# A two-layer decoder on one core: output projections, norms, the second attention's entry and the place of the weight splits

## What is computed

```python
def rms_norm(x):
    y = x * lax.rsqrt(jnp.mean(x * x, axis=-1, keepdims=True) + NORM_EPS)

for i in range(DEPTH):                                   # 2
    shift, scale, gate = silu(c) @ ada_w[i, 0] + ada_b[i, 0]   # three parts of 1024
    h = rms_norm(x) * (1.0 + scale) + shift
    y = forgetting_attention(h, ...) if i == 0 else latent_attention(h, ...)
    x = x + gate * y
    shift, scale, gate = silu(c) @ ada_w[i, 1] + ada_b[i, 1]
    h = rms_norm(x) * (1.0 + scale) + shift
    x = x + gate * conv_gated_mlp(h, ...)                # 1024 -> 2 x 2816 -> 1024
return rms_norm(x) * final_g

def latent_attention(h, w_a, g_q, g_kv, w_uq, w_ukv, w_o):
    c_q, c_kv, k_rope = jnp.split(h @ w_a, [384, 384 + 256], axis=-1)
    c_q, c_kv = rms_norm(c_q) * g_q, rms_norm(c_kv) * g_kv
    q = c_q @ w_uq       # 16 heads of 64 + 32 (rotated)
    kv = c_kv @ w_ukv    # 16 heads of 64 keys + 64 values; k_rope, rotated, is shared by all heads
    ...                  # causal softmax by blocks of 128 queries
    return o @ w_o
```

## Time and profile before

| | us |
|---|---|
| median of 3 runs (1350.25 to 1352.49) | 1351.91 |
| profiled execution | 1351.14 |
| its span | 1349.3 |

### The profile page before, as it was taken

One profiled execution on the slowest core, in us unless ns is written; L12 is line 12 of the kernel. 1 busy time (PEld: TensorE's weight loads), 2 busy tenths in 40 slices (PEclk: granted clock), 3 DMA queues, 4 the chain that ended last, 5 costly groups with the idle time before them and its releaser, 6 DMA issues.

```text
span 1349.3 us, 17962 instructions
## 1 busy us (share of the span) xinstructions
PE 1281.7 (95%) x6209; PEld 999.3 (74%) x6209; DVE 832.1 (62%) x1262; ACT 543.2 (40%) x970; POOL 9.6 (1%) x23
## 2 busy tenths in 40 slices
PE   6999999988999999999989899989899999999997
PEld 3677777666888888888867566657678888888886
DVE  3656656666888878755355666664666666663332
ACT  5544444424333333322233566553444344432222
POOL 2000000000000000000000000000000000000000
PEclk7999999997999999999979899989899999999998
DMA  9523333352556656556322111122233333333332
GB/s 307 174 63 102 118 94 94 97 185 70 182 191 195 196 176 199 161 179 193 118 76 47 34 30 35 33 72 63 63 94 93 96 102 97 93 89 102 99 90 72
DMA packets 230600, 154.29 MB, mean 114 GB/s; under 512 B 27773, under 2 KB 221778, under 8 KB 227474
## 3 DMA queue, kind: packets, MB, share of 16 engines
q1 hardware_dynamic: 230546, 153.55, 37.9%
HBM read 151.43 MB, written 2.10 MB: 114 GB/s over the span
## 4 chain that ended last, share of the span: by engine, by line
PE 86%; DVE 5%; ACT 3%; issue 2%; DMA 2%; SPq 2%; ACTq 0%; DVEq 0%
PE pj L1415 74%; PE ov L1687 3%; PE tr L1659 2%; PE sc L1643 2%; PE sc L1631 1%; DMA ada_w_sb<-in_ada_w_dram 1%; SPq L459 1%; DVE wl L966 1%; ACT wh L606 1%; DVE nmax L1120 1%; DMA first_ada<-in_ada_w_dram 1%; PE ov L1481 1%; DVE ada_w_sb L1013 1%; PE sc L1649 0%; PE ov L1573 0%
## 5 line engine op out<-in xcount | busy, mean ns | idle before, releaser
L966 DVE TENSOR_TENSOR wl<-raw,wh 128x1024 fp32r<-128x1024 f32 (+2 forms) x214 | 234.4, 1095 | 311.4 <-ACT wh L606 310.4
L1415 PE MATMUL pj<-hh,wh 128*128 128x512 f32 x992 | 402.1, 405 | 21.7 <-issue 7.0
L606 ACT ACTIVATE wh<-raw 128x1024 fp32r<-128x1024 f32 (+2 forms) x214 | 204.4, 955 | 473.2 <-PE pj L1415 473.2
L1415 PE MATMUL pj<-hh,wl 128*128 128x512 f32 x992 | 391.1, 394 | 0.0
L1415 PE MATMUL pj<-hl,wh 128*128 128x512 f32 x992 | 390.8, 394 | 0.0
L1415 PEld LDWEIGHTS pj<-hh,wh 128*128 128x128 f32 x992 | 188.6, 190 | 71.0 <-issue 16.3
L1415 PEld LDWEIGHTS pj<-hh,wl 128*128 128x128 f32 x992 | 188.8, 190 | 40.5
L1415 PEld LDWEIGHTS pj<-hl,wh 128*128 128x128 f32 x992 | 189.3, 191 | 35.8 <-DVE hl L1044 0.5
L1415 PE MATMUL pj<-gh,wh 128*128 128x512 f32 x512 | 204.3, 399 | 9.4 <-ACT tmp L797 7.2
L1415 PE MATMUL pj<-gh,wl 128*128 128x512 f32 x512 | 200.5, 392 | 0.0
L1415 PE MATMUL pj<-gl,wh 128*128 128x512 f32 x512 | 200.5, 392 | 0.0
(11 more groups left out here) (173 smaller groups left out, 1033.1 us busy)
## 6 DMA issues: line engine op xcount, KB each, us to landing
raw<-in_ffn_w_in_dram SPq DMA_DIRECT2D x88, 512.0 KB, 3.8
ada_w_sb<-in_ada_w_dram SPq DMA_DIRECT2D x40, 1024.0 KB, 5.1
raw<-in_ffn_w_out_dram SPq DMA_DIRECT2D x32, 448.0 KB, 3.6
raw<-in_fox_w_in_dram SPq DMA_DIRECT2D x24, 512.0 KB, 3.8
first_ada<-in_ada_w_dram SPq DMA_DIRECT2D x16, 512.0 KB, 8.9
raw<-in_ffn_w_out_dram SPq DMA_DIRECT2D x16, 512.0 KB, 3.9
raw<-in_fox_w_o_dram SPq DMA_DIRECT2D x8, 512.0 KB, 4.1
raw<-in_mla_w_o_dram SPq DMA_DIRECT2D x8, 512.0 KB, 3.8
```

The source lines that it names most:

```text
L606: act.activation(wh[:, n0 % 2, 0:kt, :], raw[:, n0 % 2, 0:kt, :], ACT.Copy).then_inc(w_hi, 1)
L966: dve.tensor_tensor(wl[:, n0 % 2, 0:kt, :], raw[:, n0 % 2, 0:kt, :], f32(wh[:, n0 % 2, 0:kt, :]), ALU.subtract).then_inc(w_lo, 1)
L1415: ins = pe.matmul(bank_[:, :], (wl if term == 2 else wh)[:, s, kt, :], (rl if term == 1 else rh)(kt), start=start and j == 0, stop=stop an ...
```

## The change

Seven edits.
1. Two more slices of w_ada (ten instead of eight) are done in the first attention, at other steps, and their DMAs move with them; PE's sum of the first group moves to an earlier step. In the first projection two are left, at tiles 0 and 3.
2. In both projections the first tile's residual comes ahead of the low part on DVE (`ahead`), and PE waits only for the residual, not for ACT's square.
3. `norm_over` gets ten products of constants (2, 3 and 5) into a bank that nothing reads.
4. Entry: query latents ahead of the rotated key on DVE; the spread in the middle of chunk C_KR; PE's first chunk follows the low parts tile by tile; the wait for POOL's copies moves to the second head.
5. MLA loop: the splits move from the end of b = 2 and b = 3 to their beginning, on ACT and DVE.
6. In the last pair of heads, the split of b = 3 moves to step 8.
7. `MLA_FILL` shifts one product each in two steps.

```diff
-ADA_OUT = ADA_END[1] - DT // 2
+ADA_OUT = {0: ADA_END[1] - 2, 3: ADA_END[1] - 1}
...
-MLA_FILL = (0, 3, 7, 11, 15, 19, 22, 33, 33)
+MLA_FILL = (0, 3, 7, 11, 15, 18, 21, 33, 33)
...
-FOX_ADA = {(i, 4 * j + 3): 2 * i + j for i in range(PAIRS // 2) for j in range(2)}
-FOX_ADA_LOAD = {(0, 5): 2, (1, 2): 3, (1, 5): 4, (2, 2): 5, (2, 5): 6}
-FOXO_ADA_LOAD = {2: 7, 3: 8, 4: 9, 5: 10, 6: 11}
+FOX_ADA = {(n // 8, n % 8): p for p, n in enumerate((3, 7, 10, 12, 15, 19, 22, 24, 27, 31))}
+FOX_ADA_LOAD = {(0, 5): 2, (1, 2): 3, (1, 3): 4, (1, 5): 5, (2, 2): 6, (2, 5): 7}
+FOXO_ADA_LOAD = {0: 8, 2: 9, 3: 10, 4: 11}
...
             act.activation(early[:, 7:8], eps[:, 0:1], ACT.Exp)
-            act.wait_ge(mm, C_KR + 1)
             latents_hi(QRT, KVRT)
+            split(C_KR + 2)
             act.wait_ge(kr, 2)
             act.activation(k32(0)[MQ:P, :], k32(0)[HD:MQ, :], ACT.Copy).then_inc(ev_a, 1)
-            split(C_KR + 2)
...
                 v = turned_unit(t, s)
+                if fill and b == 2:
+                    split_after(n0, t, 4, nxt)
+                if fill and b == 3 and nxt is None:
+                    split_after(n0 + 1, t, 4, nxt)
...
-                if fill and b == 2:
-                    split_after(n0, t, 4, nxt)
                 if fill and b == 3:
                     act.wait_ge(tr_r, R + (MLA_TR * j + 2))
                     mla_take_v(t * 4 + (n0 + 1))
-                    split_after(n0 + 1, t, 4, nxt)
+                if nxt is not None and s == 8:
+                    split(C_MLAO + 1)
...
-                def step(i, j, nxt):
-                    if nxt is None or j == 0:
+                def step(i, j, nxt, ahead=False):
+                    late = ahead or (nxt is not None and j == 1)
+                    if not late:
                         split_after(C + j, i, 2, nxt)
                     dve.wait_ge(mm, i * 2 + (C + j + 1))
-                    residual(i * 2 + j, j, i * 2 + (T + j), (T + j) % 2, k, norm_n)
-                    if nxt is not None and j == 1:
+                    add(i * 2 + j, (T + j) % 2, k)
+                    if late:
                         split_after(C + j, i, 2, nxt)
+                    square_add(i * 2 + j, j, i * 2 + (T + j), norm_n)
...
+            dve.wait_ge(ev_d, T_KR)
+            latents_pre(QRT, N_CQ, V_GQ)
+            latents_lo(QRT, KVRT)
+
             kt = tmp[:, 5, :]
...
+            split(C_KR + 2)
+            dve.wait_ge(kr, 1)
             dve.wait_ge(ev_d, T_KR + 1)
-            latents_pre(QRT, N_CQ, V_GQ)
-            dve.wait_ge(kr, 1)
             dve.tensor_tensor(k32(0)[HD:MQ, :], kt[0:ROPE, :], rope_sb[0:ROPE, :], ALU.add).then_inc(kr, 1)
-            latents_lo(QRT, KVRT)
-            split(C_KR + 2)
...
                 n0 = C_MLA + 2 * (j + 1)
+                if fill and b == 2:
+                    split_after(n0, t, 4, nxt)
+                if fill and b == 3 and nxt is None:
+                    split_after(n0 + 1, t, 4, nxt)
                 if s < 8:
                     maximum(s, t * 8 + (U_MLA + s), b)
...
                 mean_most(n)
+                idle_products(2)
                 mean_last(n, tile_n)
+                idle_products(3)
                 spread(n)
+                idle_products(5)
+
+            def idle_products(count):
+
+                for _ in range(count):
+                    pe.matmul(SC[0][:, :], sel[:, 0, :], sel[:, 0:QB, :], start=True, stop=True)
...
-                if (i, w) == (2, 1):
+                if (i, w) == (1, 6):
                     ada_sum(0)
...
                 def step(i, j):
-                    bank_free(i * 2 + (T + j))
+                    pe.wait_ge(ev_d, i * 2 + (T + j - 1))
                     product(C + j, i, 2, 0, 3 * DT, g_h, g_l, PJ[(T + j) % 2])
...
-            product(C_KR, 0, 0, 12, 3 * DT, h_h, h_l, PJ[T_KR % 2])
+            product(C_KR, 0, 0, 12, 15, h_h, h_l, PJ[T_KR % 2])
             spread(N_CQ)
+            product(C_KR, 0, 0, 15, 3 * DT, h_h, h_l, PJ[T_KR % 2])
...
-            pe.wait_ge(cn_lo, QRT + KVRT)
             bank_free(T_MLA)
-            product(C_MLA, 0, 0, 0, 3 * QRT, uq_h, uq_l, PJ[T_MLA % 2])
-            bank_free(T_MLA + 1)
+            for kt in range(QRT):
+                pe.wait_ge(cn_lo, KVRT + kt + 1)
+                product(C_MLA, 0, 0, 3 * kt, 3 * kt + 3, uq_h, uq_l, PJ[T_MLA % 2])
+            pe.wait_ge(ev_d, T_KR + 1)
             product(C_MLA + 1, 0, 0, 0, 3 * KVRT, ukv_h, ukv_l, PJ[(T_MLA + 1) % 2])
-            pe.wait_ge(kr_twin, 2)
...
+                    if first(t) and s == QB:
+                        pe.wait_ge(kr_twin, 2)
```

More of the change, by code:

```diff
@@ L1176, in residual, with add @@
             def residual(m, j, tile_n, bk, k, norm_n):
+                add(m, bk, k)
+                square_add(m, j, tile_n, norm_n)
+            def add(m, bk, k):
                 g = mod[:, k, 2 * DT + m:2 * DT + m + 1] if isinstance(m, int) else \
@@ L1181, in residual, with square_add @@
                                          op0=ALU.mult, op1=ALU.add).then_inc(ev_d, 1)
+            def square_add(m, j, tile_n, norm_n):
                 if isinstance(m, int) and m == DT - 1:
@@ L1198, in dense @@
                     for n in range(DT - 2):
-                        step(n // 2, n % 2, None)
-                        if ADA_OUT + n < ADA_END[1]:
-                            ada_step(ADA_OUT + n)
-                else:
-                    with dve.Fori(0, DT // 2 - 1) as i:
+                        step(n // 2, n % 2, None, n == 0)
+                        if n in ADA_OUT:
+                            ada_step(ADA_OUT[n])
+                else:
+                    for j in range(2):
+                        step(0, j, None, j == 0)
+                    with dve.Fori(1, DT // 2 - 1) as i:
                         for j in range(2):
@@ L1374, in mla_step @@
                     mla_take_k(t * 4 + (n0 + 1), 1 - j)
-                    split_after(n0, t, 4, nxt)
-                if fill and b == 3:
-                    split_after(n0 + 1, t, 4, nxt)
+                if nxt is not None and s == 8:
+                    split(C_MLAO + 1)
             for s in range(8):
```

## The result

| | before | after |
|---|---|---|
| median of 4 runs, us | 1351.35 (1350.25 to 1352.49) | 1329.86 (1328.97 to 1331.30) |
| profiled execution, its span | 1351.14, 1349.3 | 1328.97, 1327.2 |

The changed kernel takes 0.9842 of the time before (95% interval 0.9825 to 0.9859), 21.5 us less; a second series, beside other runs of the kernel before, gave 0.9857 (0.9842 to 0.9873). The forecast was 1327.8, 24.1 less. Both the time and the sign are as forecast.

A forecast was written before the change was run, and what follows sets the result against it. TensorE, busy 95% of the span, was taken as the bound, with gains only between its full stretches: 6.8 + 2.8 + 5.2 + 2.2 + 7.1 = 24.1 us less, 1327.8 us by the median; range 1318 to 1336.

The forecast's parts named there:

- First projection: First output projection: two slices left instead of four, so TensorE sets the pace, and an earlier start; 6.8 us less.
- First attention: Two more slices of w_ada moved into the first attention, taken to cost nothing because DVE has room there.
- The bound (4.8): Cost of the two added slices in the first attention if their cover is gone: 2 x 2.4 us.
- Norms: Products of constants in three norms fill TensorE's idle time and partly hold its clock; 2.8 us less, between +1.5 and -5.5.
- half of 5.5: Share taken of the three norms' 5.5 us at most, since constants fill somewhat over half of TensorE's idle time.
- Entry: Entry of the second attention: earlier spread and query latents ahead of rope work; 5.2 us less, bounds 5.6 and 4.0.
- The 0.4 us that I took off: At the second attention's entry: POOL's copies beside the next weight slice's low part stretch it from 0.56 to 0.96 us.
- Loop: Second attention's loop of head pairs: splits ahead of softmax work; 2.2 us less, between 12 and -4.
- Last two heads and second projection: Second attention's end and the projection behind: earlier splits, and TensorE's wait at the third slice goes; 5.65 + 1.45 = 7.1 us less.
- (a): Rival: granted clock still falls in the norms, at the entry and in the last heads; 1335 us, chance 0.20.
- (b): Rival: splits ahead cost nothing in the second attention's loop and all 12 us come; 1318 us, chance 0.12.
- (c): Rival: slower, two close waits make the clock fall in each of eight loop heads; 1355 us, chance 0.03.

## Why the prediction was right, and where it was off

**First projection: right, 6.8 against 6.6.** The chain that ended last, in the changed kernel, has no slice and no DMA between the third tile and the norm. Start, us, what:

```profile
265.89 25.42 PE pj L1433 x111
291.31 0.97 PE ov L1529 x8
292.28 5.66 PE pj L1433 x24
297.94 0.79 PE tr L1542 x8
298.73 5.62 PE pj L1433 x24
```

In the kernel before, slices and their DMAs stand on it. The third tile starts at 269.28, the mean at 304.17, so 34.89 against the 34.7 worked out. The start moved by 1.22 (forecast 1.2); undone alone it is 1.24. The residual now runs from 266.73, beside ACT's high part (266.81), and the low part from 267.90. TensorE starts when that is done, and the wait of the earlier trace rows is gone.

**First attention: the step that failed.** The prediction took nothing for two more slices, since DVE works about 4 of each step's 6.5 us. That is a mean over four steps. A slice in a pair's third step stands ahead of the fourth block's maxima, the longest there are, and ACT and PE wait for these. Measured 1.5 us for ten slices. When two of them move by one step, 1.67 us go, so the other eight and the sum of the gate cost nothing in all (two pairs also trade a microsecond: with the old places the fourth is 0.99 shorter and the fifth 1.19 longer). "The step is followed by one with room" was the wrong way round: the next step's maximum was already due. The bound (4.8) held it.

**Norms: the size right, in part by luck, for a reason only half right.** 2.7 measured, 2.8 taken as half of 5.5. The half was meant as "they hold the clock in part". The runs say what part: the fall is shorter (0.57 to 0.68 in 16 us without constants, 0.79 to 1.00 with them), and in some executions there is none. The sign that the prediction asked for, a clock of 1.00 through the norms, came at two of three.

What the prediction had wrong is the price of a fall. It counted a microsecond at the spread and another at the tiles' end, where the low part and the next high part are late. The first is real, about 0.9, wherever the fall meets the whole spread. The second, 0.4 to 0.7, came only where the clock was still low some 11 to 12 us behind the spread's start: in five of the six norms without constants. Behind the MLP the kernel before loses both, 1.60 against the changed kernel. Behind the second projection its spread took 1.18, so that its 0.7 there is the tiles' end alone. The sixth, behind the MLP in the kernel without constants, had the clock back after 9.0 us and lost 0.86, the spread's part. With these constants the clock was back by 9 us in every trace, and the second part never came: DVE's 1.45 us a tile sets the pace at either clock. With more of them it was once back only after 10.2 us, and 0.2 was lost.

The norm behind the first projection gained only 0.4 over the kernel before: its spread takes 2.08 in the changed kernel, too, as in the earlier trace rows. There the kernel without constants was no slower at all: its spread took 1.26 in that execution, and the tiles' end 0.6.

So the sum depends on the execution. Against the kernel before, the three norms, each taken up to the next spread, are together 1.4 to 3.0 us shorter in the eleven traces with these constants, 3.5 with more of them, and 0.6 shorter in the one without any. That the first profile gave 2.7 is luck.

**Entry: right, 5.2 against 5.4.** TensorE's three waits behind the spread, where one of 6.17 was the earlier trace rows; the prediction asked for three of about 1 us, and the last is 1.68:

```profile
734.32 0.47 PE L1433 MATMUL pj<-hh,wh 128*128 128x512 f32 x1 [0.92 <-issue]
737.35 0.47 PE L1433 MATMUL pj<-gh,wh 128*128 128x512 f32 x1 [0.71 <-DVE wl L968]
740.66 0.47 PE L1433 MATMUL pj<-hh,wh 128*128 128x512 f32 x1 [1.68 <-DVE soft L1361]
```

And what stood for POOL's part, from the timeline of the same stretch:

```profile
733.42 1.89 DVE L1323 TENSOR_TENSOR hl<-tmp,hh 128x512 fp32r<-128x512 f32 x3
...
737.98 1.27 POOL L594 COPY soft<-soft 32x512 f32<-32x512 f32 x2 [729.11 <-DVE soft L1356]
...
739.16 0.56 DVE L968 TENSOR_TENSOR wl<-raw,wh 128x384 fp32r<-128x384 f32 x1 [1.24 <-ACT wh L606]
```

Three subtractions take 1.89 us without POOL beside them, 2.72 with it. The 0.4 us that I took off for a stretched split didn't come: the split took 0.56, what it takes elsewhere. POOL's two copies took 2.15 beside the subtractions and 1.27 alone, and had ended by 739.25 when the split had hardly begun. With the old entry both numbers come back, 2.72 and 2.15, in another kernel. I had carried over the slowed duration of the copies.

The means hide how it goes. Nanoseconds of one instruction (least, median, most), DVE's subtraction and POOL's copy, before and after:

```profile
L1310 DVE TENSOR_TENSOR hl<-tmp,hh x3: 692/1091/1097, 744.3 to 745.9; 128x512 fp32r<-128x512 f32 x3
L594 POOL COPY soft<-soft x2: 962/1044/1126, 744.3 to 745.5; 32x512 f32<-32x512 f32 x2
```

```profile
L1323 DVE TENSOR_TENSOR hl<-tmp,hh x3: 683/684/685, 733.4 to 734.6; 128x512 fp32r<-128x512 f32 x3
L594 POOL COPY soft<-soft x2: 603/607/611, 738.0 to 738.6; 32x512 f32<-32x512 f32 x2
```

The subtraction that started 0.03 us ahead of the first copy wasn't slowed (0.69 us); the two behind it took 0.4 longer, and so did the copies (0.5 and 0.35). That looks like two engines that take turns, each instruction waiting for the other engine's, and not like a common slowing; only two traces show it. It agrees with what the Trainium skill, GPSIMD Engine Reference, section 1 "Specifications", states of shared SBUF interfaces and contention with VectorE instructions that have two SBUF inputs; that section names no size.

**Loop: the mechanism right, one term too small.** Forecast 2.2, measured 1.2. With T the transposes of a head without output products (772.10 in the changed kernel), the working stands as follows against these lines:

```profile
772.10 0.61 PE L1685 MATMUL tr<-ident,diag 128*128 128x128 f32 x4
...
774.16 0.52 ACT L606 ACTIVATE wh<-raw 128x384 fp32r<-128x384 f32 x1
...
775.96 0.35 DVE L1132 TENSOR_SCALAR tmp<-tmp,rinv 128x256 f32<-128x256 f32 x1
...
778.37 0.42 DVE L1387 COPY soft<-tr 128x256 f32<-128x256 f32 x1
...
781.25 0.61 PE L1685 MATMUL tr<-ident,diag 128*128 128x128 f32 x4
```

High part at T+2.06 (2.07 worked out), scaling ended at T+4.21 (4.22), TensorE's wait for it 0.75. From there it parts: the next product comes at T+5.19 (fence above), not T+4.46, of which 0.44 is the edge of PE's loop. Before the change, that edge lay under a wait for the low part, and so had no row of its own. The copy of v ended at T+6.69 (6.64 worked out), but TensorE came later than it, so the 0.5 us wait for it did not arise. The next head is at T+9.15, not 8.98: 0.65 lost instead of 0.48, against 0.94 won in a head with output products (forecast 0.97). Six periods give 1.95 and the first pair takes 0.79 back. I named the right wait in the place of the removed one, and missed that a cost hidden under the removed wait appears with it. The larger lesson is one that the prediction had in its hands: it priced the two kinds of heads at +0.48 and -0.97, and placing the splits by kind is worth 4.4 us.

**Last two heads and second projection: right, 7.1 against 6.9.** The waits of 2.59 and 2.29 us became these, at a clock of 1.00:

```profile
885.50 0.55 PE L1685 MATMUL tr<-ident,tmp 128*128 128x128 f32 x3 [1.09 <-DVE soft L1387]
...
887.54 0.63 PE L1685 MATMUL tr<-ident,diag 128*128 128x128 f32 x4 [0.30 <-DVE diag L1132]
```

One of 1.09 is just over what I asked for, "none over 1 us". Those of the last head are 0.49 and 0.18, where the sum had 0.7 and 0.6. The total is right, but no run isolates the clock's part in it (1.8 us in the sum, 2.65 as a bound): with the old splits back, the clock fell for half as long and 5.13 of 5.55 us were there.

**Rivals.** (a), the clock not held, came about at the norms in some executions. At the entry and in the last heads it did not come about in any trace with the new order of that stage, and it fell there in each trace with the old one (the kernel before, and the kernel with the old entry or the old last pair). So at those two places the order of the work decides by these traces, unlike in the norms. (b) is out: the splits ahead are not free, and even placed by kind they give 5.5 of its 12 us. (c) is out, the clock is 1.00 through the loop. The range of 1318 to 1336 holds the time.

**Start and end.** 0.4 and 0.5 us of the difference lie ahead of the first attention and behind the last norm. The first output products start anywhere between 90.4 and 92.3 us in these traces of kernels that are alike up to there, and what lies behind the last norm takes 13.6 to 15.4, so neither is shown to be the change's.

## What to carry to other kernels

Place an insertion by what is queued behind it at that step, not by the engine's mean load: 2.5 us on DVE cost nothing one step later and 0.9 us here. When a loop alternates two kinds of bodies, price the edit for each kind and apply it only where it wins; here that was worth more (4.4 us on top) than the edit everywhere (1.3). Measure such things by the distance of instructions at a stage's edges, which repeats within 0.1 to 0.2 us where the granted clock is the same; medians scatter by one or two.

## What the runs showed of the hardware that I had not expected

Whether TensorE's clock falls from 2.4 to 1.2 GHz in a norm is not decided by the program alone: two executions of the changed kernel had 0.89, 1.00, 1.00 and 0.89, 0.89, 0.89 there. With constants it fell though TensorE was idle for less than 1 us at a time around the spreads. The products of constants went with a shorter fall in all twelve traces that have them. They cost no time of their own where the engine waits anyway: from the mean's last products to the spread it is 2.30 us with and without them.

A loop's edge on PE took 0.44 us between two groups of products where nothing hid it, and the profile booked it as a wait for DVE.

POOL and DVE hold each other up: a copy on POOL took 0.96 and 1.13 us instead of 0.61 beside DVE's subtractions, and a subtraction 1.09 instead of 0.68 beside the copies, except for the one that had started first.
